# Expert rows gathered and scattered by indirect DMAs through HBM, in place of 0/1 products

## The chip, the cores and the metric

The kernel runs on one core of one Trainium2 chip. The metric is the device time of one execution in microseconds (us). An engine's work is told as the profile names it: PE is TensorE, DVE is VectorE, ACT is ScalarE, POOL is GpSimd, SP is SyncE, which here only issues DMAs.

## The reference, cut to what matters

The model has two layers. In each, 384 tokens (128 of a prompt, 256 latent ones) of width 1024 go through a mixer (pooling, attention, convolution) and then through a mixture of experts, which is where the change lies. A token is sent to 2 of 32 experts, both in the group that its router picks:

```python
g_w, g_idx = lax.top_k(softmax(t @ router_grp + b), 1)          # 1 of 4 groups
top_v, top_i = lax.top_k(e_logits[of that group], 2)            # 2 of its 8 experts
w = g_w * softmax(top_v)
h = silu(t @ w_gate[e]) * (t @ w_up[e])                         # 1024 -> 256
y = sum over both experts of  w * (h @ w_down[e])               # 256 -> 1024
x = layer_norm(ALPHA * x + gate2 * y)
```

All is float32. With the reference's inputs its routing gives, in the first layer, all 32 experts some rows, one of them more than 64 (72); in the second layer one expert has no row and three have more than 64 (87, 100 and 71).

## The kernel before

A token-expert assignment is a pair; there are 768. Pairs are sorted by expert. A chunk is up to 64 rows of one expert, and the list of chunks is made on the chip from the router's counts: `chunk_tab` holds each chunk's expert and its first column. Here it has 33 and 34 chunks, which the loops round up to 34 in each layer.

**Routing.** PE makes ranks of the pairs by products with a triangle of ones (`ranks_ready`, L870 and L872). VectorE turns them into sorted places `s1`, `s2` and builds the 0/1 matrix `Pm` (tokens by pairs, L1520 and L1521). **Gather.** PE multiplies the token rows `urow` by `Pm` (L907, 48 products), ScalarE and VectorE copy the result to `XsT`, the sorted rows as columns. Between, VectorE builds the weighted matrix `Pw` (L1575 to L1577), PE turns it (L892) and ScalarE stores it as `PTw`. SP waits for the chunk list (`chunks_ready`) and only then loads experts, each 3 MB (gate, up and down) into one of four slots of `ring`.

**Chunk loop.** For a chunk: `gate_up` (L928, 16 float32 products, each of two passes), silu by ScalarE (L1205), the product with the up half by VectorE (L1609), one transpose (L938), its copy to `hT` (L1611), `down` (L943), ScalarE's copy `take` to `yrow` (L1200), four transposes back to columns (L954) and a copy to `YsT` (L1618). In a round of four chunks PE issues gate_up of chunk i before down of chunk i-1, and ScalarE's silu of chunk i stands before its take of chunk i-1. Next to the copies, VectorE copies the inputs of a later chunk out of `XsT` (L1599). A slot is freed when down has read it, and SP then issues the next load into it.

**Unsort.** After the loop PE turns `YsT` to rows `Ysr` (L981) and multiplies them by `PTw` (L990, 48 products), which weights each pair and adds a token's two. VectorE adds this to the residual (L1446), PE sums for the layer norm (L822 and L827). The loads of the next layer's `w_mod` go on meanwhile.

Buffers of chunks alternate by `i % 2`, and semaphores that count chunks tell each engine when it may go on.

Of the kernel before, what the change touches and what calls it, by code (L numbers as in the profile page):

```python
# [25 lines left out]
ds = bass.ds  # L26
# [29 lines left out]
PADDED = PAIRS + W  # L56
# [9 lines left out]
MAX_CHUNKS = NE + (PAIRS - NE) // W  # L66
MAX_ROUNDS = -(-MAX_CHUNKS // RING)
LISTED = MAX_ROUNDS * RING + 2
# [17 lines left out]
for _name, _n in VECS:  # L86
# [4 lines left out]
              ("rank", NE), ("kk", 1), ("rounds", MAX_ROUNDS), ("inv", 2 * POOL_N)]  # L91


def shape_constants():
# [21 lines left out]
    c["kk"] = np.arange(P)[:, None]  # L116
    c["rounds"] = np.tile(np.arange(MAX_ROUNDS) * RING, (P, 1))
# [8 lines left out]
    iota = np.concatenate([np.tile(np.arange(PAIRS), (P, 1)), c["tri"]], axis=1).astype(np.float32)  # L126
    lam = np.array([0.8 - 0.6 * math.exp(-0.3 * l) for l in range(DEPTH)])
    lam = np.stack([lam, 1.0 - lam], axis=-1)[:, None, :].repeat(P, axis=1).astype(np.float32)
    return table, iota, lam
# [28 lines left out]
DVE_STEPS = 208  # L158


def build(nc, g, consts, iota_dram, lam_dram, y_prompt, y_sample, new_k, new_v):
    with ExitStack() as ctx:
# [11 lines left out]
        XS = max(KD * PADDED, NT * (D + PAIRS) + 2 * PAIRS)  # L174
        arena = sb("arena", [P, 2 * XS])
        PTw = sb("PTw", [P, ST, T])
# [18 lines left out]

        chunk_tab = sb("chunk_tab", [1, 2, LISTED], I32)
        rounds_tab = sb("rounds_tab", [1, 2, DEPTH], I32)
        before_f = sb("before_f", [1, 2, DEPTH + 1])
        before_tab = sb("before_tab", [1, 2, DEPTH + 1], I32)
# [36 lines left out]
        ptflat = PTw[:].rearrange("p s t -> p (s t)")  # L236
        sumX = ptflat[:, 0:2 * POOL_COLS].rearrange("p (c n) -> p c n", c=2)
        sumY = ptflat[:, 2 * POOL_COLS:4 * POOL_COLS].rearrange("p (c n) -> p c n", c=2)
        mrow = arena[:, 0:2 * HALF].rearrange("p (b n) -> p b n", b=2)

        XsT = arena[:, 0:KD * PADDED].rearrange("p (k n) -> p k n", k=KD)
        YsT = arena[:, XS:XS + KD * PADDED].rearrange("p (k n) -> p k n", k=KD)
        Ysr = arena[:, 0:ST * D].rearrange("p (s n) -> p s n", s=ST)
        urow = arena[:, XS:XS + NT * D].rearrange("p (t n) -> p t n", t=NT)
        Pm = arena[:, XS + NT * D:XS + NT * D + NT * PAIRS].rearrange("p (t n) -> p t n", t=NT)
        Pw = arena[:, XS + NT * (D + PAIRS):XS + NT * (D + PAIRS) + 2 * PAIRS].rearrange("p (t n) -> p t n", t=2)
        assert XS + NT * (D + PAIRS) + 2 * PAIRS <= 2 * XS
# [3 lines left out]
        sg = arena[:, KD * PADDED:KD * PADDED + FF].rearrange("p (b n) -> p b n", b=2)  # L251
        hrow = arena[:, XS + KD * PADDED:XS + KD * PADDED + FF].rearrange("p (b n) -> p b n", b=2)
        assert KD * PADDED + FF <= XS and 2 * W == P and FF == 2 * P
        hT = krow[:, 0:FF].rearrange("p (b n) -> p b n", b=2)
        iota_tri = tail[:, PAIRS:2 * PAIRS + P]
        iota, tri = iota_tri[:, 0:PAIRS], iota_tri[:, PAIRS:]
# [3 lines left out]
        RT_COLS = NT * (NG + NE) + NT * NG + 4 * NT * NE  # L260
# [10 lines left out]
        o1, o2 = rts(NT, NE), rts(NT, NE)  # L271
        etmp, asg = rts(NT, NE), rts(NT, NE)
        r3 = sb("r3", [P, 15, NT])
        gmax, gsum, gw, m1, m2, cm, q, s1, s2, w1, w2, rq, gcm, c1, c2 = [r3[:, i, :] for i in range(15)]
        assert at[0] == RT_COLS
        asg_flat = asg.rearrange("p t n -> p (t n)")
        lgT = arena[0:NG + NE, RT_COLS:RT_COLS + T]

        tot, start, cb, le, dd, ce = [tail[:, 2 * PAIRS + P + (NE + 1) * i:2 * PAIRS + P + (NE + 1) * (i + 1)] for i in range(6)]
        gtmp = tail[:, 2 * PAIRS + P + 6 * (NE + 1):][:, 0:NT * NG].rearrange("p (a b) -> p a b", a=NT)  # L280
        chk = sb("chk", [P, 4])
        small = sb("small", [P, 2, 2, 4])
        rnd = sb("rnd", [P, MAX_ROUNDS + 3])
# [27 lines left out]
        iota_loaded = signal("iota_loaded", 1, 16)  # L311
# [71 lines left out]
        chunk_cols = signal("chunk_columns", 1)  # L383
        chunk_turned = signal("chunk_turned", 1)
        chunks_ready = signal("chunk_list", 1)
        P_ready = signal("gather_matrix", 2 * NT)
        Pw_ready = signal("weighted_matrix", NT)
        Pw_turned = signal("weighted_turned", 2 * NT)
        PT_ready = signal("unsort_matrix", 2 * NT)
        gath_ready = signal("gathered", 2 * KD)  # L390
        xs_act = signal("sorted_x_act", KD)
        xs_dve = signal("sorted_x_dve", KD)


        xc_ready = signal("chunk_x_copied", 0)
        gu_ready = signal("gate_up_ready", 0, credit=4)
# [6 lines left out]
        y_turned = signal("y_turned", 0, credit=2)  # L403
        y_placed = signal("y_placed", 0, credit=2)
        ys_turned = signal("ys_turned", 12, credit=1)
        ys_act = signal("ys_rows_act", 6)
        ys_dve = signal("ys_rows_dve", 6)
# [1263 lines left out]
```

## Time and profile before

| what | value |
|---|---|
| median of 3 runs | 1259.55 us (1258.58 to 1259.93) |
| span of the profiled execution | 1257.7 us |
| PE busy (matmuls) | 1063.3 us, 85% |
| DVE, ACT, POOL busy | 419.7, 284.7, 32.8 us |
| moved by DMA | 300.36 MB, mean 239 GB/s |
| expert loads | 68 of each kind, 1024 KB each |

The profiled execution's own time is its span, 1257.7 us, and the median of the runs lies 1.85 us over it, for what surrounds the span. The page's chain of work says for each stretch of the span what it waited for last; windows give busy time by stretch. A busy PE is not a fast one: the chain and the gaps in the timeline tell what a stage really waits for.

### The profile page before, as it was taken

Reading aid. Unit: us, or ns where it says so; the run is one execution under the profiler, and the core shown is the slowest. Engines: PE = TensorE matmul, PEld = TensorE weight load, DVE = VectorE, ACT = ScalarE, POOL = GpSimd, SP = SyncE. Lnnn points to the kernel's source line nnn. Section 1 sums busy time; section 2 is a strip of 40 time slices with the busy share of each in tenths; the row PEclk is TensorE's granted clock in tenths of the full one; section 3 lists DMA queues with packets and bytes.
Section 4 is the critical chain, followed back from the end, with each engine's and each line's share of the span. In section 5 each row is a group of like instructions: output and inputs, shape, how many; then the busy total and the mean of one; then the engine's idle time right before and its main releaser. Section 6 shows DMA issues by size and latency. Waiting matters only on the chain.

```text
span 1257.7 us, 17279 instructions
## 1 busy us (share of the span) xinstructions
PE 1063.3 (85%) x5662; PEld 605.6 (48%) x5663; DVE 419.7 (33%) x1031; ACT 284.7 (23%) x638; POOL 32.8 (3%) x62
## 2 busy tenths in 40 slices
PE   2699988967888888888979998897789888888893
PEld 1256456534544444445535645653454444444552
DVE  0138553156122222223242854414712222222313
ACT  1200056042111111112050005704221111111304
POOL 4000000010000000000020000000000000000000
PEclk8799989988999999999989998998899999999997
DMA  9962530003799999996457244000189999999201
GB/s 344 394 227 87 193 122 1 1 16 115 314 418 419 416 417 419 418 417 264 188 170 300 101 164 154 2 0 15 72 331 403 417 418 418 417 417 419 94 1 50
DMA packets 70966, 300.36 MB, mean 239 GB/s; under 512 B 5381, under 2 KB 9763, under 8 KB 53505
## 3 DMA queue, kind: packets, MB, share of 16 engines
q1 hardware_dynamic: 68144, 293.98, 58.7%
q0 software_dynamic: 2768, 5.71, 1.4%
q8 instruction: 28, 0.46, 0.2%
q14 instruction: 26, 0.21, 0.1%
HBM read 297.05 MB, written 2.62 MB: 238 GB/s over the span
## 4 chain that ended last, share of the span: by engine, by line
PE 65%; DMA 20%; DVE 6%; issue 3%; SPq 3%; ACT 2%; DVEq 0%; ACTq 0%; POOL 0%
DMA ring<-in_w_down 17%; PE ps L660 12%; PE ps L928 9%; PE ps L943 7%; PE ps L840 7%; PE ps L907 5%; PE ps L990 5%; PE ps L663 3%; PE ps L625 3%; PE ps L827 2%; SPq L475 2%; DMA ring<-in_w_mod 2%; PE ps L822 2%; PE ps L954 1%; PE ps L762 1%
## 5 line engine op out<-in xcount | busy, mean ns | idle before, releaser
L928 PE MATMUL ps<-ring,tail 128*64 128x256 f32 x2176 | 248.5, 384 | 23.8 <-DMA ring<-in_w_down 14.6
L928 PEld LDWEIGHTS ps<-ring,tail 128*64 128x64 f32 x2176 | 166.0, 138 | 105.0 <-issue 43.5
L660 PE MATMUL ps<-uT,ring 128*128 128x384 f32 x448 | 152.5, 499 | 6.6 <-DMA ring<-in_w_in 5.0
L943 PE MATMUL ps<-ring,krow 128*64 128x512 f32 x544 | 131.7, 605 | 26.1 <-DVE krow L1611 26.1
L660 PEld LDWEIGHTS ps<-uT,ring 128*128 128x128 f32 x448 | 86.7, 195 | 64.8 <-issue 5.9
L1200 ACT ACTIVATE tail<-ps 128x512 f32<-128x512 f32 x68 | 40.6, 597 | 183.2 <-PE ps L943 183.2
L1611 DVE COPY krow<-ps 128x128 f32<-128x128 f32 x68 | 19.8, 292 | 176.9 <-PE ps L938 176.9
L907 PE MATMUL ps<-arena 128*128 128x512 f32 (+1 forms) x192 | 67.4, 507 | 11.5 <-DVE arena L1521 11.5
L1618 DVE COPY arena<-ps 128x512 f32 x68 | 47.1, 692 | 86.8 <-PE ps L954 86.8
L1446 DVE SCALAR_TENSOR_TENSOR uT<-ps,modT,uT 128x128 f32<-128x128 f32 x64 | 23.8, 413 | 148.9 <-PE ps L840 88.7
L625 PE MATMUL ps<-ring,sT 128*32 128x384 f32 x512 | 47.9, 530 | 27.7 <-DMA ring<-in_w_mod 24.2
L943 PEld LDWEIGHTS ps<-ring,krow 128*64 128x64 f32 x544 | 33.0, 136 | 77.9 <-DVE krow L1611 39.0
L1323 DVE SCALAR_TENSOR_TENSOR arena<-arena,dw 128x414 f32<-128x414 f32 x118 | 67.6, 646 | 0.0
L990 PE MATMUL ps<-PTw,arena 128*128 128x384 f32 x192 | 64.4, 487 | 1.8 <-DVE arena L1638 1.8
L840 PE MATMUL ps<-arena,ring 128*128 128x384 f32 x192 | 63.6, 486 | 0.0
L1205 ACT ACTIVATE arena<-ps 128x128 f32<-128x128 f32 x68 | 18.8, 277 | 163.6 <-PE ps L928 163.4
L907 PEld LDWEIGHTS ps<-arena 128*128 128x128 f32 x192 | 37.1, 198 | 38.1 <-issue 23.8
L954 PEld LDWEIGHTS ps<-cst,tail 128*128 128x128 f32 x272 | 28.5, 141 | 49.1 <-issue 40.6
L1147 ACT ACTIVATE arena<-uT 128x384 f32<-128x384 f32 x32 | 15.1, 523 | 157.3 <-DVE uT L1452 157.3
L990 PEld LDWEIGHTS ps<-PTw,arena 128*128 128x128 f32 x192 | 36.3, 190 | 27.1 <-ACT arena L1219 2.2
L840 PEld LDWEIGHTS ps<-arena,ring 128*128 128x128 f32 x192 | 36.5, 190 | 25.4
L954 PE MATMUL ps<-cst,tail 128*128 128x128 f32 x272 | 44.6, 287 | 4.2 <-ACT tail L1200 4.2
(257 smaller groups left out, 1009.2 us busy)
## 6 DMA issues: line engine op xcount, KB each, us to landing
ring<-in_w_gate SPq DMA_DIRECT2D x68, 1024.0 KB, 10.7
ring<-in_w_up SPq DMA_DIRECT2D x68, 1024.0 KB, 12.8
ring<-in_w_down SPq DMA_DIRECT2D x68, 1024.0 KB, 14.9
ring<-in_w_mod SPq DMA_DIRECT2D x32, 1536.0 KB, 10.9
ring<-in_w_in SPq DMA_DIRECT2D x8, 1536.0 KB, 15.1
ring<-in_w_out SPq DMA_DIRECT2D x4, 1536.0 KB, 19.0
ring<-in_w_in SPq DMA_DIRECT2D x2, 2048.0 KB, 13.1
ring<-in_w_in SPq DMA_DIRECT2D x4, 512.0 KB, 12.7
```

The lines of the kernel that those rows point to most:

```text
L625: last = mm(ps[32 * g_:32 * (g_ + 1), bank, 0:HALF], both, slot[s][:, k, (g_ % 2) * HALF:(g_ % 2 + 1) * HALF], start=(k == 0), stop=(k == ...
L660: last = mm(ps[:, n % 4, 0:T], slot[s][:, k, c:c + P], uT[:, k, :], start=(k == 0), stop=(k == KD - 1))
L663: last = mm(ps[:, n % 4, 0:AW], uT[:, k, rows * P:(rows + 1) * P], slot[s][:, k, c:c + AW], start=(k == 0), stop=(k == KD - 1))
L840: last = mm(ps[:, m % 4, 0:T], wt, mixT[:, k, :], start=(k == 0), stop=(k == KD - 1))
L907: last = mm(ps[:, n % 4, 0:b - a], urow[:, t, k * P:(k + 1) * P], Pm[:, t, a:b], start=(t == 0), stop=(t == NT - 1))
L928: last = mm(ps[W * half:W * (half + 1), i % 2, 0:2 * P].rearrange("p (j f) -> p j f", j=2), xc[:, i % 2, k, :], gate_up_w[i][:, :, k, half ...
L943: last = mm(ps[W * half:W * (half + 1), 3 + i % 2, :], hT[:, i % 2, f * W:(f + 1) * W], down_w[i][:, f, half * 512:(half + 1) * 512], star ...
L954: last = tr(ps[:, 5 + i % 2, c * P:(c + 1) * P], yrow[:, i % 2, c * P:(c + 1) * P], ident)
L990: last = mm(ps[:, m % 4, 0:T], Ysr[:, s, m * P:(m + 1) * P], PTw[:, s, :], start=(s == 0), stop=(s == ST - 1))
L1200: fn(yrow[:, i % 2, :], ps[:, 3 + i % 2, :], ID).then_inc(y_rows.sem, 1)
L1323: conv_own.append(own.add(v.scalar_tensor_tensor(cacc[:, c, :], src, wt, cacc[:, c, :], ALU.mult, ALU.add)))
L1618: v.tensor_copy(YsT[:, :, ds(off, W)].rearrange("p (h c) n -> p h c n", h=2), ps[:, 5 + i % 2, :].rearrange("p (c h n) -> p h c n", c=4, h ...
```

## The change

The 0/1 products go. Token rows are stored to a scratch in HBM, `u_rows` (768 rows of 512 floats, so a token has two). Two products of one-hot matrices (L938 of the new kernel) make `row_idx`: for each chunk the row numbers to read and the row numbers of `y_pairs` to write; places without a pair get a number out of bounds, which the DMA skips. For each chunk GpSimd issues one indirect DMA that fetches up to 128 half rows into `xg` (`fetch`) and one that writes `yrow` to `y_pairs` (`put`). PE turns `xg` to columns (`turn_x`, four transposes), in place of the four that turned y. After the loop ScalarE's queue loads `y_pairs` (3 DMAs of 1 MB), VectorE weights and adds a token's two rows, PE turns the sum (24 transposes), and the residual follows as before.

The chunk list becomes fixed: experts 0 to 31 in eight rounds of four, whether they have rows or not, and SP may load them before routing is known. Rows over 64 of an expert go to extra chunks, in turns of two; at least one turn runs. The loop over layers is written out. In the main loop PE's, ScalarE's and GpSimd's part read:

```diff
+def fetch(idx, done, half, i):                      # GpSimd
+    pool.wait_ge(x_turned.sem, done + (i + 1))
+    pool.nop(nofuse=True)
+    pool.indirect_dma_start(xg[:, i % 2, :], None, u_rows, bass.IndirectOffsetOnAxis(ap=idx, axis=0),
+                            bounds_check=2 * T - 1, oob_is_err=False).then_inc(xg_loaded[i % 2].sem, 16)
+def put(idx, done, half, i, first=False):
+    pool.wait_ge(y_rows.sem, done + (i + 3))
+    pool.nop(nofuse=True)
+    pool.indirect_dma_start(y_pairs, bass.IndirectOffsetOnAxis(ap=idx, axis=0), yrow[:, i % 2, :], None,
+                            bounds_check=4 * T - 1, oob_is_err=False).then_inc(y_stored[i % 2].sem, 16)
+def freed(half, i):
+    pool.wait_ge(y_stored[i % 2].sem, (half + (i // 2 + 1)) * 16)
+    pool.sem_inc(y_free.sem, 1)
+for i in range(2):
+    fetch(row_idx[:, i:i + 1], done, half, i)
+for i in range(NE):
+    if i + 2 < NE:
+        fetch(row_idx[:, i + 2:i + 3], done, half, i + 2)
+    put(row_idx[:, CHUNKS + i:CHUNKS + i + 1], done, half, i)
+    if i >= 1:
+        freed(half, i - 1)
...
+def chunk(done, half, used, i, ahead, follow):      # PE
+    turn_h(done, i)
+    if ahead:
+        turn_x(done, half, i + 2)
+    down(done, i, i % RING)
+    if follow:
+        gate_up(done, used((i + 1) % RING) + (i + 1) // RING, i + 1, (i + 1) % RING)
...
+with act.Fori(0, MAIN_ROUNDS - 1) as r:             # ScalarE
+    for i in range(RING):
+        silu(done + r * RING, i + 1)
+        take(done + r * RING, lambda s: slot_before(s) + r, i)
...
+with pool.Fori(0, turns) as r:                      # extra chunks, GpSimd
+    for i in range(2):
+        nc.gpsimd.tensor_copy(extra_idx[:, i, 0:1], row_idx[:, ds(NE + (r * 2 + i), 1)])
+        nc.gpsimd.tensor_copy(extra_idx[:, i, 1:2], row_idx[:, ds(CHUNKS + NE + (r * 2 + i), 1)])
...
+for t in range(NT):                                 # ScalarE's queue, then VectorE
+    act.dma_start(yk[:, t, :], y_pairs.rearrange("(t q r) n -> t q (r n)", t=NT, r=4)[t]).then_inc(y_loaded[t].sem, 16)
...
+    step(v.tensor_scalar(ysum[:, t, :], yk[:, t, D:2 * D], w2[:, t:t + 1], None, ALU.mult))
+    v.scalar_tensor_tensor(ysum[:, t, :], yk[:, t, 0:D], w1[:, t:t + 1], ysum[:, t, :], ALU.mult, ALU.add)
```

PE in the middle of a round, before: gate_up of chunk 2, then the transpose (L938) and down (L943) of chunk 1, the transposes of y (L954) of chunk 0, then gate_up of chunk 3.

```order
L924 REGISTER_ALU [waits expert_loaded2]
L928 MATMUL ps<-ring,tail 64x256 [waits h_rows_ready,chunk_x_copied]
L928 MATMUL ps<-ring,tail 64x256 x15
L936 REGISTER_ALU
L938 MATMUL ps<-cst,arena 128x128 [waits h_columns_ready,h_rows_ready]
L943 MATMUL ps<-ring,krow 64x512 [waits y_rows_copied,h_columns_ready]
L943 MATMUL ps<-ring,krow 64x512 x3
L954 MATMUL ps<-cst,tail 128x128 [waits y_placed,y_rows_copied]
L954 MATMUL ps<-cst,tail 128x128 x3
L924 REGISTER_ALU [waits expert_loaded3]
L928 MATMUL ps<-ring,tail 64x256 [waits h_rows_ready,chunk_x_copied]
```

And in the new kernel: gate_up of chunk 2 (L959), then the transpose (L968) of the same chunk, the transposes of x (L949) of the chunk two further on, down (L976) of chunk 2, and gate_up of chunk 3.

```order
L955 REGISTER_ALU [waits expert_loaded2]
L959 MATMUL ps<-ring,tail 64x256 [waits h_rows_ready,chunk_x_copied]
L959 MATMUL ps<-ring,tail 64x256 x15
L968 MATMUL ps<-cst,arena 128x128 [waits h_columns_ready,h_rows_ready]
L946 ISA
L949 MATMUL ps<-cst,pool_sums 128x128 [waits chunk_x_copied,chunk_x_rows0]
L949 MATMUL ps<-cst,pool_sums 128x128 x3
L976 MATMUL ps<-ring,krow 64x512 [waits y_rows_copied,h_columns_ready]
L976 MATMUL ps<-ring,krow 64x512 x3
L955 REGISTER_ALU [waits expert_loaded3]
L959 MATMUL ps<-ring,tail 64x256 [waits h_rows_ready,chunk_x_copied]
```

Between a chunk's gate_up and its own down no longer stands another chunk's gate_up, and the transposes of x, which wait for a fetch (`chunk_x_rows0`), stand ahead of down.

ScalarE in the new kernel: silu (L1208) of the next chunk, then take (L1215) of this one, whose down PE has ended before that next gate_up. Before, the order of the two in the code was the same, but take's down was issued after the gate_up of the silu ahead of it.

```order
L1206 REGISTER_ALU
L1208 ACTIVATE arena<-ps 128x128 [waits h_rows_ready,gate_up_ready]
L1215 ACTIVATE tail<-ps 128x512 [waits y_rows_free,slot_done2,down_half_ready]
L1206 REGISTER_ALU
L1208 ACTIVATE arena<-ps 128x128 [waits h_rows_ready,gate_up_ready]
L1213 REGISTER_ALU [waits down_half_ready]
L1215 ACTIVATE tail<-ps 128x512 [waits y_rows_free,slot_done3]
```

GpSimd in the new kernel has all fetches (L593) and puts (L600) in one row, one of each for a chunk: the fetch of chunk i+2, then the put of chunk i. Before, it had no instruction in this stage.

```order
L593 DMA pool_sums<-u_rows,row_idx 128x512 [waits y_rows_stored0,chunk_x_turned]
L600 DMA y_pairs<-tail,row_idx 1536x512 [waits y_rows_copied]
L593 DMA pool_sums<-u_rows,row_idx 128x512 [waits y_rows_stored1,chunk_x_turned]
L600 DMA y_pairs<-tail,row_idx 1536x512 [waits y_rows_copied]
L593 DMA pool_sums<-u_rows,row_idx 128x512 [waits y_rows_stored0,chunk_x_turned]
L600 DMA y_pairs<-tail,row_idx 1536x512 [waits y_rows_copied]
```

What moved: a fetch stands behind the put of the chunk three before its own.

## Rows read from the trace of the kernel before

**Rows 1.** The page: span, part 4 by engine, one group of part 5.

```profile
span 1257.7 us, 17279 instructions
...
PE 65%; DMA 20%; DVE 6%; issue 3%; SPq 3%; ACT 2%; DVEq 0%; ACTq 0%; POOL 0%
...
L1618 DVE COPY arena<-ps 128x512 f32 x68 | 47.1, 692 | 86.8 <-PE ps L954 86.8
```

**Rows 2.** Windows: busy us of each engine, granted clock, DMA share, GB/s.

```profile
389.00:569.00 180.00, 154.34 (x1082) 84.41 (x1082) 39.12 (x97) 28.68 (x54) 0.00 (x0) 1.00 1.02 418
```

**Rows 3.** The chain that ended last, in order of time: start, us, what.

```profile
330.74 8.56 PE ps L928 x64
...
348.50 3.60 PE ps L928 x32
...
448.14 18.09 DMA ring<-in_w_down
...
478.29 18.04 DMA ring<-in_w_down
...
579.35 1.95 PE ps L943 x7
...
625.99 0.93 PE ps L822 x2
...
1180.45 1.94 PE ps L943 x8
```

**Rows 4.** The timeline of one stretch of the chunk loop: start, us, engine, line.

```profile
474.09 0.28 DVE L1609 TENSOR_TENSOR arena<-arena,ps 128x128 f32<-128x128 f32 x1
...
474.42 0.33 PE L938 MATMUL ps<-cst,arena 128*128 128x128 f32 x1 [1.08 <-DVE arena L1609]
474.79 0.29 DVE L1611 COPY krow<-ps 128x128 f32<-128x128 f32 x1 [0.42 <-PE ps L938]
...
475.13 1.94 PE L943 MATMUL ps<-ring,krow 128*64 128x512 f32 x8 [0.38 <-DVE krow L1611]
...
477.00 0.66 PE L954 MATMUL ps<-cst,tail 128*128 128x128 f32 x4
477.24 0.60 ACT L1200 ACTIVATE tail<-ps 128x512 f32<-128x512 f32 x1 [3.72 <-PE ps L943]
...
483.83 0.28 ACT L1205 ACTIVATE arena<-ps 128x128 f32<-128x128 f32 x1
484.14 0.29 DVE L1609 TENSOR_TENSOR arena<-arena,ps 128x128 f32<-128x128 f32 x1 [4.75 <-ACT arena L1205]
```

**Rows 5.** The timeline: a VectorE step, rank product, row of 768, residual.

```profile
284.16 0.26 DVE L1485 TENSOR_TENSOR arena<-arena,cst 128x96 f32<-128x96 f32 x1
...
285.65 1.15 PE L872 MATMUL ps<-arena,cst 128*128 128x96 f32 x6
...
305.50 0.96 DVE L1577 TENSOR_TENSOR arena<-arena,tail 128x768 f32<-128x768 f32 x1
...
594.24 0.74 DVE L1446 SCALAR_TENSOR_TENSOR uT<-ps,modT,uT 128x128 f32<-128x128 f32 x2 [4.37 <-PE ps L990]
```

**Rows 6.** The timeline of GpSimd, and the copy that released it.

```profile
647.63 0.91 POOL L559 DMA_DIRECT2D router_w<-in_router_grp  x1
...
1245.42 0.60 ACT L1229 ACTIVATE arena<-ps 128x512 f32<-128x512 f32 x1 [0.26 <-PE ps L1002]
...
1246.31 0.54 POOL L577 DMA_DIRECT2D out<-arena  x1 [389.43 <-ACT arena L1229]
```

**Rows 7.** DMA issues at 250:265 and 640:655: count, KB each, us to landing.

```profile
vec_rows<-in_conv_ln_b POOLq DMA_DIRECT2D x1, 1.0 KB, 1.6
...
arena<-in_cache_k POOLq DMA_DIRECT2D x1, 256.0 KB, 3.0
...
conv_pw<-in_conv_pw POOLq DMA_DIRECT2D x1, 256.0 KB, 6.3
router_w<-in_router_exp POOLq DMA_DIRECT2D x1, 128.0 KB, 6.6
```

More of the change, by code:

```diff
@@ L55 @@
 W = 64
-PADDED = PAIRS + W
 RING = 4
@@ L90 @@
 CONST_COLS = [("ident", P), ("ones", P), ("rot", P), ("cos", LAT), ("sin", LAT),
-              ("rank", NE), ("kk", 1), ("rounds", MAX_ROUNDS), ("inv", 2 * POOL_N)]
+              ("rank", NE), ("turns", MAX_TURNS), ("inv", 2 * POOL_N), ("tri", P), ("place", P),
+              ("chunk", CHUNKS), ("sixty_fours", STEPS_64), ("tok", 2 * NT), ("tok_rank", 2 * NT), ("row", 1)]
 def shape_constants():
@@ L976, in _ @@
[L976 to L985 removed]
+                wait(idx_ready, l, 1)
@@ new lines, in _ @@
+                gate_up(done, slot_before(0), 0, 0)
+                with pe.Fori(0, MAIN_ROUNDS - 1) as r:
+                    for i in range(RING):
+                        chunk(done + r * RING, half + r * (RING // 2), lambda s: slot_before(s) + r, i, True, True)
+                last_done, last_half = done + (NE - RING), half + (NE - RING) // 2
+                for i in range(RING):
+                    chunk(last_done, last_half, lambda s: slot_before(s) + (MAIN_ROUNDS - 1), i, i + 2 < RING, i + 1 < RING)
@@ new lines, in _ @@
+                wait(chunks_ready, l, 1)
+                turns = turns_now(pe, l)
+                with pe.Fori(0, turns) as r:
+                    at_done, at_half = before * RING + NE + (turns_before + r) * 2, (before * RING + NE) // 2 + (turns_before + r)
+                    used = lambda s: slot_before(s) + (MAIN_ROUNDS + r)
+                    for i in range(2):
+                        turn_x(at_done, at_half, i)
+                    gate_up(at_done, used(0), 0, 0)
+                    for i in range(2):
+                        chunk(at_done, at_half, used, i, False, i == 0)
@@ L986, in _ @@
+                wait(y_sum, l, NT)
                 for m in range(KD):
@@ new lines, in _ @@
+                for i in range(RING):
+                    if i + 1 < RING:
+                        silu(done + (NE - RING), i + 1)
+                    take(done + (NE - RING), lambda s: slot_before(s) + (MAIN_ROUNDS - 1), i)
+                wait(chunks_ready, l, 1)
+                turns = turns_now(act, l)
+                with act.Fori(0, turns) as r:
+                    at_done = before * RING + NE + (turns_before + r) * 2
+                    silu(at_done, 0)
+                    silu(at_done, 1)
+                    for i in range(2):
+                        take(at_done, lambda s: slot_before(s) + (MAIN_ROUNDS + r), i)
@@ L1220, in _ @@
+                for b in range(2):
+                    act.wait_ge(y_stored[b].sem, ((before * RING + NE) // 2 + (turns_before + turns)) * 16)
+                for t in range(NT):
+                    act.dma_start(yk[:, t, :], y_pairs.rearrange("(t q r) n -> t q (r n)", t=NT, r=4)[t]).then_inc(y_loaded[t].sem, 16)
                 scale_x()
@@ new lines, in chunk @@
+                def chunk(done, i, ahead, follow):
+                    columns(done, i)
+                    if ahead:
+                        copy_x(done, i + 2)
+                    if follow:
+                        hidden(done, i + 1)
+                done = before * RING + turns_before * 2
+                for i in range(2):
+                    copy_x(done, i)
+                hidden(done, 0)
+                with dve.Fori(0, MAIN_ROUNDS - 1) as r:
+                    for i in range(RING):
+                        chunk(done + r * RING, i, True, True)
@@ new lines, in _ @@
+                for i in range(RING):
+                    chunk(done + (NE - RING), i, i + 2 < RING, i + 1 < RING)
+                wait(chunks_ready, l, 1)
+                turns = turns_now(dve, l)
+                with dve.Fori(0, turns) as r:
+                    at_done = before * RING + NE + (turns_before + r) * 2
+                    for i in range(2):
+                        copy_x(at_done, i)
+                    hidden(at_done, 0)
+                    for i in range(2):
+                        chunk(at_done, i, False, i == 0)
```

589 lines of the change are left out of this document (250 added, 339 removed).

## The prediction

> **What bounds the kernel now.** I read the page, then the chain of waits, then windows, then the timeline of the chunk loop. The page gives the span, 1257.7 us, with PE on 65% of the chain and DMA on 20% [rows 1]. The 68 copies of L1618 [rows 1] are 68 chunks, 34 a layer. The chain [rows 3] shows the expert stage of the first layer: the loop begins at 330.7 and its last down ends at 581.3, 250.6 us; then come the unsort and the layer norm, whose first sums end at 626.9, 45.6 us later. The last down of the second layer ends 601.1 us after that of the first, so the second repeats the first. Inside the loop the same wait for `ring<-in_w_down` comes every 30.15 us [rows 3]: four chunks, 7.54 us each. The window says why: DMA share 1.02 at 418 GB/s [rows 2], and 3.146 MB at 418 GB/s take 7.53 us. So the loop is bound by weight loads, but PE is close behind, busy 154.3 of 180 us there. A change can gain ahead of the loop and behind it; within it, it can only keep 7.5 us a chunk or lose.
>
> **Ahead of the loop.** The rank product ends at 286.8 [rows 5]. New until the first gate_up: some 20 steps of VectorE, 13 small ones at 0.26 us, six of 192 to 264 elements that I put at 0.45, one of 768 at 0.96 [rows 5], together 6.5 us with some overlap; 12 passes on PE, by 1.15 us for six [rows 5] 2.3 us; three steps, 0.9; GpSimd's start 0.29 after its release (1246.31 less the copy's end, 1246.02) [rows 6]; a fetch of up to 256 KB, 3.0 us when nothing else runs [rows 7]; 0.9 more for the second one's issue; four transposes 0.66 [rows 4] and a copy 0.69 [rows 1]. The loop starts near 301, not 330.7: a gain of 29.7 us a layer. The weights of four chunks are in by then, since SP no longer waits for the list.
>
> **A chunk in the loop.** PE alone: gate_up 3.60 [rows 3]; then silu and the product until PE starts, 483.83 to 484.43 and 0.05, that is 0.65; the transpose 0.33, the four of x 0.66 (the copy to `hT` lies under them), down 1.94 [rows 4]. Sum 7.2 us, which alone would cost nothing against 7.54. But the order of the new kernel closes a ring. fetch(i+3) stands on GpSimd behind put(i); put(i) waits for take(i); take(i) stands on ScalarE behind silu(i+1), which waits for gate_up(i+1). PE needs fetch(i+3) two small steps later, ahead of down(i+1), and everything of PE is queued behind that wait. Counted from the end of gate_up(i+1): silu and take 0.96 with their gaps (0.28 and 0.60 [rows 4]), GpSimd's start 0.29 [rows 6], the issue of put, the fetch from its start to landing, 0.05 to PE. PE arrives at 0.65 + 0.33 = 0.98. The stall is 0.3 us plus put's issue plus the fetch.
>
> Neither indirect DMA is in the trace. Put's issue: a plain one takes 0.54 us, one of 1024 pieces 0.91 [rows 6]; I take 0.91, as addresses must be read one by one. The fetch: 1.6 us for 1 KB on a quiet chip, 3.0 for 256 KB just before a weight load, 6.3 and 6.6 beside one [rows 7]. A freed slot's load starts with the end of down and takes 7.5 us; the fetch starts 3.6 + 0.96 + 0.3 + 0.9 = 5.8 us after that, so it runs beside the load for its first half only, and about a third of its rows exist: I take 4.0. The stall is then 0.3 + 0.9 + 4.0 = 5.2 us, with bounds of 0.3 + 0.5 + 1.6 = 2.4 and 0.3 + 0.9 + 6.6 = 7.8.
>
> For the fetch there is a page's price. The Trainium skill, "DMA: Bandwidth & Descriptors", section "Anatomy of one DMA", gives GpSimd's DMAs a fixed cost of about 2.0 us plus the bytes at 436 GB/s, which makes 2.6 us for 256 KB; the trace has 3.0 to 6.6. By the page the stall would be 3.8 us and the time, as an estimate, 1427 us.
>
> It comes 29 times a layer (chunks 3 to 31; the first three are fetched early, the last two chunks have none behind them). Main loop: 32 x 7.2 + 29 x 5.2 = 381 us. Weights cost nothing here, as 7.5 us of load fit into 12.4. VectorE's copies of x take the place of those to `YsT`, of the same size.
>
> **Extra chunks.** The first layer has one, the second three, so one turn and two turns of two chunks. A turn starts only when all puts have landed: take 0.6, put 0.3 + 4.0, the count read 1.0, four small copies 0.8, GpSimd's start 0.3 and two fetches 4.9, transposes and copy 1.35: 13.3 us in which PE stands. (The two small costs are estimates, by the smallest steps [rows 4, 5].) Then two chunks without overlap, 3.60 + 0.65 + 0.33 + 0.34 + 1.94 = 6.9 each. A turn is 27 us.
>
> **Behind the loop.** From the last down: take and put 4.9, ScalarE's issue 0.4, then 3 MB. Alone these are 2.5 us each at 418 GB/s after 2 us, the last at 9.5; in the first layer they share the DMA engines with 12 MB of `w_mod`, so I double the 2.5: 17. The last weighted sum is two steps over 1024 elements, by 0.96 for 768 [rows 5] 2.6 us. The eight turned tiles are paced by 0.74 of VectorE [rows 5] and 0.5 + 0.93 of PE [rows 3, 4], 1.5 each, 12. So 36.9 us in the first layer and 29.4 in the second, against 45.6: 8.7 and 16.2 gained.
>
> **The sum.** First layer: 381.4 + 27 - 250.6 = +157.8. Second: 381.4 + 54 - 250.6 = +184.8. Ahead: 2 x -29.7 = -59.4. Behind: -24.9. Together +258.3, span 1516.0; the median stood 1.85 over the span, so 1518 us.
>
> **Rivals.**
> - The stall is hidden and the loop stays bound by weights. For it: PE has 7.2 us of own work against 7.54. 28 further loads at 7.53 plus the rows (768 pairs, 4 KB each way, 6.3 MB a layer, 0.44 us a chunk) end the loop 144 us a layer earlier than above: 1230 us, faster. It decides where put's issue and the fetch together stay under about 0.5 us (258.3 over 58 stalls is 4.45 us off the 5.2). The smallest rows give 2.1. Chance 0.03.
> - Cheap DMAs: tiny ones as on a quiet chip, stall 2.4. 58 x 2.8 = 162, and 16 from three turns: 1340 us. For it: two thirds of the rows are skipped. Against it: any fetch with data on the DMA engines took 3.0. Chance 0.08 for all below 1400.
> - Dear DMAs: the fetch is as slow as beside a load, 6.6, stall 7.8: 58 x 2.6 + 16 more, 1685 us. If GpSimd needs twice 0.91 for each index list, 52 and more on top, 1740. For it: the indices lie in 128 partitions, and no row shows what that costs. Chance 0.17 for above 1620.
> - My forecast, 1400 to 1620 us: 0.72.
>
> **How the numbers follow.** The forecast is the likeliest case. The range 1400 to 1690 leaves out both lower cases (0.11) and the end of the dear one (0.07). A measurement here tells 0.2% from no change; every case but the first is slower, so faster 0.03, same 0.01, slower 0.96.
>
> **What the profile after would show.** If the ring is right: in the chain a repeated sequence of gate_up, silu, take, put, fetch, transposes, down; PE idle some 5 us a chunk ahead of the transposes of x, released by the DMA into `pool_sums`; a round of four near 50 us; DMA at about 60% in the loop and 250 GB/s, not 418; GpSimd busy about 2 us a chunk. The loop starts near 301, the first turn shows PE idle for 13 us. The forecast is wrong if PE's wait stands elsewhere, if rounds stay at 30 us, if GpSimd itself is busy most of the period, or if skipped rows cost as much as real ones.

## The result, and the profile after

The changed kernel took 1699.6 us (median of 4 runs) against 1259.7 us: a ratio of 1.350 (95% interval 1.348 to 1.352). The forecast was 1518 us with a range up to 1690; the sign and the place were right, the size was not. One of the four runs of experiment 1, 1327.6 us, lies over 1.5% above its fastest and is left out of its figures; with it the median is 1307.9 us, from which the expectation of experiment 5 starts. The page of the kernel after, its span, chain by engine, and the group of the transposes of x (busy us, mean ns of one, idle time before it and what ended most of it), to set beside [rows 1]:

```profile
span 1696.7 us, 14958 instructions
...
PE 60%; DMA 19%; issue 7%; DVE 4%; ACT 4%; POOL 3%; SPq 2%; POOLq 1%; ACTq 0%; DVEq 0%
...
L949 PE MATMUL ps<-cst,pool_sums 128*128 128x128 f32 x280 | 76.5, 429 | 405.0 <-DMA pool_sums<-u_rows,row_idx 372.1
```

405 us of PE's idle time stand ahead of one line, and 372 of them are ended by the gather into `pool_sums`. So the added time has an address. The window over the main loop of the first layer, to set beside [rows 2]:

```profile
332.00:770.00 438.00, 242.84 (x1298) 116.68 (x1299) 35.60 (x84) 21.76 (x56) 57.49 (x57) 0.72 0.56 218
```

The DMA share is 0.56 in place of 1.02 and 218 GB/s in place of 418: the weights no longer bound the loop. GpSimd, the last of the five pairs, is busy 57 of 438 us, so no engine bounds it either; it is a ring of waits. The figure behind the pairs, the granted clock, is 0.72, and it was 1.00 before. The chain of the kernel after, from the end of one gate_up to the next (start, us, what), where the chain of before had `ring<-in_w_down` every 30.15 us [rows 3]:

```profile
439.26 0.05 ACT arena L1208
439.43 0.04 issue
439.48 0.61 ACT tail L1215
440.18 0.53 issue
440.73 0.07 issue
440.92 1.01 POOL y_pairs L600
441.93 0.30 issue
442.24 4.46 DMA pool_sums<-u_rows,row_idx
446.69 0.04 issue
446.74 1.11 PE ps L949 x4
```

This is the ring that the prediction named, read from top to bottom: SiLU, take, put, fetch, transposes. Three of its pieces can be laid beside the forecast's. Between the take's end (439.48 + 0.61 = 440.09) and the put's start (440.92) lie 0.83 us, not 0.29. The put's issue is 1.01 us, not 0.91, and 0.30 us follow it before the fetch starts. The fetch lands 4.46 us after its start here (5.13 in the chunk before, median 4.3 over the loop, 3.6 to 5.1), against 4.0.

The fourth piece is PE itself. Windows of the chunk before this one (length, busy us of PE, PEld, DVE, ACT and POOL, granted clock, DMA share, GB/s): the wait, the transposes with the first half of down, its second half, and the two halves of gate_up.

```profile
423.90:430.80 6.90, 0.00 (x0) 0.00 (x0) 0.26 (x1) 0.00 (x0) 2.02 (x2) 0.61 0.89 353
430.90:433.00 2.10, 2.10 (x8) 1.15 (x10) 0.69 (x1) 0.00 (x0) 0.00 (x0) 0.50 0.00 0
433.00:435.40 2.40, 2.40 (x10) 0.55 (x8) 0.00 (x0) 0.00 (x0) 0.00 (x0) 0.50 0.00 0
435.40:437.40 2.00, 2.00 (x20) 1.35 (x18) 0.00 (x0) 0.00 (x0) 0.00 (x0) 0.94 0.20 25
437.40:439.40 2.00, 1.73 (x17) 0.84 (x12) 0.00 (x0) 0.14 (x1) 0.00 (x0) 1.00 0.96 397
```

PE's timeline in the same stretch, the transposes and down:

```profile
430.88 1.11 PE L949 MATMUL ps<-cst,pool_sums 128*128 128x128 f32 x4 [7.04 <-DMA pool_sums<-u_rows,row_idx]
431.92 3.68 PE L976 MATMUL ps<-ring,krow 128*64 128x512 f32 x8
```

In the 6.9 us in which PE stands the granted clock falls to its lower level, 1.2 GHz (0.61 is the mean of the wait, 0.50 the figure of its last 4.9 us), and it stays there through the transposes and nearly all of down; it is back at 2.4 GHz in gate_up. The down products took 3.68 us here and 1.94 before [rows 4], the transposes 1.11 and 0.66. No DMA runs beside them (share 0.00), so it is not traffic that slows them. So the wait is paid a second time, in the work behind it.

The rest, from the timeline of PE:

| | forecast | measured |
|---|---|---|
| first gate_up of the first layer | 301 | 302.4 |
| main loop, first gate_up to last down | 381, 381 | 471.6, 475.3 |
| turn of the first layer | 27 | 26.2 |
| two turns of the second | 54 | 57.5 |
| last down to the last sum of the norm | 36.9, 29.4 | 37.8, 27.6 |
| from there to the first gate_up of the second layer (304.5 before) | 274.8 | 265.8 |

The two main loops are 184 us over their terms. The other differences nearly cancel, and the miss is 182: the second layer's first gate_up comes 9 us sooner than forecast, the rest is up to 3.5 us a line. A chunk with a stall takes 15.5 us (29 of them from 311.1 to 760.2), not 12.4.

### The profile page after: what moved, and what is told of

Its sections match the earlier page's. It is cut to its first block, busy times and chain, and to the rows that moved or that the text cites. A ratio compares the mean times of both kernels' runs of the same rounds, so it can differ in the third digit from the quotient of the medians.

```text
span 1696.7 us, 14958 instructions
## 1 busy us (share of the span) xinstructions
PE 1075.4 (63%) x5304; PEld 573.3 (34%) x5304; DVE 369.6 (22%) x890; ACT 241.1 (14%) x587; POOL 180.2 (11%) x219
## 3 DMA queue, kind: packets, MB, share of 16 engines
q0 software_dynamic: 14672, 20.57, 3.4%
## 4 chain that ended last, share of the span: by engine, by line
PE 60%; DMA 19%; issue 7%; DVE 4%; ACT 4%; POOL 3%; SPq 2%; POOLq 1%; ACTq 0%; DVEq 0%
PE ps L959 16%; DMA pool_sums<-u_rows,row_idx 15%; PE ps L976 13%; PE ps L721 9%; PE ps L901 5%; PE ps L949 4%; POOL y_pairs L600 3%; PE ps L724 2%; ACT tail L1215 2%; PE ps L686 2%; SPq L483 1%; DMA arena<-y_pairs 1%; PE ps L883 1%; PE ps L888 1%; DMA ring<-in_w_mod 1%
## 5 line engine op out<-in xcount | busy, mean ns | idle before, releaser
L949 PE MATMUL ps<-cst,pool_sums 128*128 128x128 f32 x280 | 76.5, 429 | 405.0 <-DMA pool_sums<-u_rows,row_idx 372.1
L959 PE MATMUL ps<-ring,tail 128*64 128x256 f32 x2240 | 275.3, 402 | 0.0
L976 PE MATMUL ps<-ring,krow 128*64 128x512 f32 x560 | 223.6, 944 | 3.8 <-DVE krow L1593 3.8
L959 PEld LDWEIGHTS ps<-ring,tail 128*64 128x64 f32 x2240 | 172.1, 150 | 151.3 <-issue 83.1
L949 PEld LDWEIGHTS ps<-cst,pool_sums 128*128 128x128 f32 x280 | 49.6, 215 | 420.6 <-DMA pool_sums<-u_rows,row_idx 373.3
L1208 ACT ACTIVATE arena<-ps 128x128 f32<-128x128 f32 x70 | 19.4, 278 | 971.0 <-PE ps L959 971.0
L600 POOL DMA_INDIRECT y_pairs<-tail,row_idx x64 | 64.6, 1010 | 808.6 <-ACT tail L1215 781.1
L1581 DVE COPY tail<-ps 128x512 f32<-128x512 f32 x70 | 48.4, 692 | 462.5 <-PE ps L949 462.5
L1588 DVE TENSOR_TENSOR arena<-arena,ps 128x128 f32<-128x128 f32 x70 | 20.1, 288 | 455.2 <-ACT arena L1208 455.2
L976 PEld LDWEIGHTS ps<-ring,krow 128*64 128x64 f32 x560 | 50.4, 204 | 103.6 <-issue 97.5
L593 POOL DMA_INDIRECT pool_sums<-u_rows,row_idx x64 | 65.0, 1016 | 42.9 <-issue 28.9
L968 PE MATMUL ps<-cst,arena 128*128 128x128 f32 x70 | 22.9, 327 | 55.4 <-DVE arena L1588 55.4
L1215 ACT ACTIVATE tail<-ps 128x512 f32<-128x512 f32 x70 | 41.5, 593 | 13.3 <-PE ps L976 13.3
L724 PE MATMUL ps<-ring,uT 128*128 128x512 f32 x96 | 42.1, 594 | 0.0
L968 PEld LDWEIGHTS ps<-cst,arena 128*128 128x128 f32 x70 | 9.7, 138 | 87.1 <-DVE arena L1588 67.3
## 6 DMA issues: line engine op xcount, KB each, us to landing
ring<-in_w_in SPq DMA_DIRECT2D x2, 2048.0 KB, 11.3
```

The costliest lines, as they stand in the source:

```text
L593: pool.indirect_dma_start(xg[:, i % 2, :], None, u_rows, bass.IndirectOffsetOnAxis(ap=idx, axis=0), bounds_check=2 * T - 1, oob_is_err=Fal ...
L600: pool.indirect_dma_start(y_pairs, bass.IndirectOffsetOnAxis(ap=idx, axis=0), yrow[:, i % 2, :], None, bounds_check=4 * T - 1, oob_is_err= ...
L724: last = mm(ps[:, n % 4, 0:AW], uT[:, k, rows * P:(rows + 1) * P], slot[s][:, k, c:c + AW], start=(k == 0), stop=(k == KD - 1))
L949: last = tr(ps[:, 5 + i % 2, c * P:(c + 1) * P], xg[:, i % 2, c * P:(c + 1) * P], ident)
L959: last = mm(ps[W * half:W * (half + 1), i % 2, 0:2 * P].rearrange("p (j f) -> p j f", j=2), xc[:, i % 2, k, :], gate_up_w[s][:, :, k, half ...
L976: last = mm(ps[W * half:W * (half + 1), 3 + i % 2, :], hT[:, i % 2, f * W:(f + 1) * W], down_w[s][:, f, half * 512:(half + 1) * 512], star ...
```

## The experiments

Times "alone" are a single run beside runs of the kernel before; the others are medians of four, in experiment 1 of three. In the diffs, `silu`, `take`, `fetch` and `put` are the calls of the prediction.

**1. The ring cut on GpSimd.** Three chunks are fetched at the start, and fetch(i+3) stands ahead of put(i).

```diff
-    if i + 2 < NE:
-        fetch(row_idx[:, i + 2:i + 3], done, half, i + 2)
+    if i + 3 < NE:
+        fetch(row_idx[:, i + 3:i + 4], done, half, i + 3)
     put(row_idx[:, CHUNKS + i:CHUNKS + i + 1], done, half, i)
```

> GpSimd issues the fetch of chunk i+3 ahead of the put of chunk i instead of behind it; nothing else differs. Theory A (the ring put, fetch, transposes, down, gate_up, take, put sets the pace): the fetch has a whole chunk more, the stall of 7.0 us ahead of the transposes of x goes, the loop is bound by weights again at 7.5 to 8.0 us a chunk, the main loop takes 240 to 255 us instead of 471 and the median falls to 1235 to 1265 us. Rival B (indirect DMAs are slow or disturb the weight loads whatever the order): the DMA engines or GpSimd stay the bound, over 10 us a chunk, over 1400 us.

Measured: 1304.6 us, ratio 1.037 (1.031 to 1.043), above the 1235 to 1265 of theory A and far below rival B's 1400. One reordered call takes away 395 us of the 440 with the same DMAs in it: their order was the cause. But it isn't the kernel without a ring. GpSimd's timeline there:

```profile
425.78 1.01 POOL L600 DMA_INDIRECT y_pairs<-tail,row_idx  x1 [8.06 <-PE ps L949]
427.10 1.01 POOL L593 DMA_INDIRECT pool_sums<-u_rows,row_idx  x1 [0.30 <-issue]
432.61 1.01 POOL L600 DMA_INDIRECT y_pairs<-tail,row_idx  x1 [4.50 <-DMA y_pairs<-tail,row_idx]
433.92 1.01 POOL L593 DMA_INDIRECT pool_sums<-u_rows,row_idx  x1 [0.31 <-issue]
443.25 1.01 POOL L600 DMA_INDIRECT y_pairs<-tail,row_idx  x1 [8.32 <-PE ps L949]
444.56 1.01 POOL L593 DMA_INDIRECT pool_sums<-u_rows,row_idx  x1 [0.30 <-issue]
```

The brackets give the idle time before and what the profile takes for its end. For the puts they mislead: the chain has the take ahead of them (424.34 to 424.95 for the put of 425.78), with the same 0.83 us between. So a fetch still starts right behind a late put each time, and the fetch of 427.10 landed only at 433.97, as it now runs beside a weight load (median 6.4 us, where it was 4.3). Chunks alternate: one goes through in 6.9 us, the next waits and takes 10 or 11.

**2. The take ahead of the SiLU,** GpSimd's order as in the changed kernel. ScalarE copies the rows of chunk i out while PE does gate_up(i+1).

```diff
-    silu(done + r * RING, i + 1)
     take(done + r * RING, lambda s: slot_before(s) + r, i)
+    silu(done + r * RING, i + 1)
```

> ScalarE copies y of chunk i (take) ahead of the silu of chunk i+1; GpSimd's order stays as in the changed kernel. Theory A: the ring loses gate_up and silu, the put starts about 4 us earlier, the stall shrinks from 7.0 to about 3 us: 29 x 2 x 4 = 233 us less and some of the slow clock back, 1400 to 1460 us. Rival B: no more than 20 us less, since the DMAs themselves set the pace.

Measured: 1598.0 us alone, above the 1400 to 1460 expected. The put starts 1.6 us after the end of down in place of 5.3, but the chunk falls only from 15.5 to 13.7 us: the fetch now starts 2.7 us after the first issue of the weight load (427.20 and 424.55) instead of 6.4 (442.24 and 435.86), and its median landing is 6.3 us. The transfer moved beside another gives back 2.0 of the 3.7 us that the move gains.

**3. PE kept busy in the wait.** Twelve products of 128x256 that nothing reads, ahead of the wait for the gathered rows; nothing else changes.

```diff
     pe.wait_ge(xc_ready.sem, done + (i + 1))
+    for _ in range(12):
+        mm(ps[:, 5 + i % 2, 0:LAT], ident, C["cos"], start=True, stop=True)
     pe.wait_ge(xg_loaded[i % 2].sem, (half + (i // 2 + 1)) * 16)
```

> The changed kernel, with 12 products of no use (128x128 by 256 columns, into a bank that the transposes overwrite) put on PE ahead of each wait for a fetch in the main loop, 5.2 us at the full clock, less than the stall of 7.0. Theory C (PE stands, the granted clock falls to half, and about 1.1 us of each chunk's 15.4 are PE's own work at the slower clock): the clock stays near 1.0, down takes 1.94 us again instead of up to 3.7, a chunk takes 14.2 to 14.6 us, 1620 to 1655 us. Rival D (the slow down and gate_up come of contention with DMA writes, not of the clock): durations stay, and the time is 1697 or more.

Measured: 1604.8 us alone, 95 less than the changed kernel, by adding work; theory C holds, and its 1620 to 1655 was too cautious. PE's timeline after the wait:

```profile
439.44 0.66 PE L951 MATMUL ps<-cst,pool_sums 128*128 128x128 f32 x4 [1.44 <-DMA pool_sums<-u_rows,row_idx]
440.03 1.94 PE L978 MATMUL ps<-ring,krow 128*64 128x512 f32 x8
```

Transposes and down are back at the times of [rows 4], and the window 332 to 700 has a granted clock of 0.99. A chunk takes 13.7 us (29 from 315.2 to 712.9). The 1.8 us between this and 15.5 are what the full clock gives back, some 104 us in 58 chunks; 10 of them are lost again in the first chunk of each layer, where the useless products stand and no wait was. The wait for the gather stays.

**4. Plain DMAs in place of the indirect ones.** Put and fetch move 128 fixed rows each. The experts get other tokens' rows, so the output isn't the reference's.

```diff
-    pool.indirect_dma_start(xg[:, i % 2, :], None, u_rows, ...)
+    pool.dma_start(xg[:, i % 2, :], u_rows[0:P, :])
```

> Fetch and put are plain GpSimd DMAs of 128 fixed rows, in the same places and with the same waits; the experts so get rows that are not theirs, and all 128 rows of a chunk move instead of about a third. Theory A with the index list as a small term: put's issue 0.54 us instead of 1.01, the fetch's issue likewise, its landing a little later for three times the bytes: 0.5 to 1.0 us a chunk less, 1640 to 1680 us. Rival E (the index lists are the dear part): the fetch lands in 2.5 us or less and the time falls below 1600.

Measured: 1744.1 us alone, slower than the changed kernel. The timeline of ScalarE's copy and of GpSimd in this kernel:

```profile
445.20 0.60 ACT L1213 ACTIVATE tail<-ps 128x512 f32<-128x512 f32 x1
...
446.34 0.54 POOL L599 DMA_DIRECT2D y_pairs<-tail  x1 [14.10 <-ACT tail L1213]
446.92 0.54 POOL L593 DMA_DIRECT2D pool_sums<-u_rows  x1
```

And its DMA issues in the window 340 to 700 (count, KB each, median us to landing):

```profile
y_pairs<-tail POOLq DMA_DIRECT2D x22, 256.0 KB, 6.1
pool_sums<-u_rows POOLq DMA_DIRECT2D x22, 256.0 KB, 6.0
```

The issue is 0.54 instead of 1.01 us and the gap of 0.30 is gone, 0.74 us less from the put's start to the fetch's; the put itself starts 0.54 us after the copy in place of 0.83. But the landing goes from 4.3 to 6.0, which is more than both savings. My expectation held the issue for the larger of the two and was wrong. So the index lists are not what made the changed kernel slow. Whether the longer landing comes from the bytes (each DMA moves all 256 KB) or from the earlier start (5.3 us after the load's first issue, 446.92 and 441.66, in place of 6.4), this run doesn't separate; experiment 10 bears on it.

**5. Both reorderings,** with two buffers.

> Both reorderings at once: GpSimd gathers chunk i+3 ahead of putting chunk i back, and ScalarE copies the rows of a chunk out ahead of the next chunk's SiLU. With the gather first alone the median was 1307.9 us and the chunks alternated between 6.9 and 10.5 us. Theory P: the gathers still queue behind puts on GpSimd, and the puts are late because the copy waits behind the SiLU; then an earlier copy moves the loop towards the weights' own 7.5 to 8.3 us per chunk: 1265 to 1285 us. Theory Q: the two buffers of gathered rows are what holds (a gather can't start before the chunk two before it is turned, and lands 6 to 8 us later beside the weights); then an earlier copy changes little: 1298 to 1312 us.

Measured: 1269.2 us, ratio 1.008 (1.006 to 1.010). The earlier copy, worth 102 us by itself, is worth 35 here. Theory P holds: the puts were late, and the two buffers were enough.

**6 and 7. Four buffers of gathered rows,** in order of the changed kernel on ScalarE (6) and with the earlier copy (7). Two of them lie in a part of `arena` that is free during the loop; fetch(i+4) waits for the turn of chunk i.

```diff
-    fetch(row_idx[:, i + 2:i + 3], done, half, i + 2)
+    fetch(row_idx[:, i + 4:i + 5], done, i + 3, i + 4)
     put(row_idx[:, CHUNKS + i:CHUNKS + i + 1], done, half, i)
```

> Four buffers of gathered rows in place of two, and four gathers issued ahead: gather i+4 waits for the turn of chunk i and stands ahead of put i on GpSimd. ScalarE's order as in the changed kernel. Theory Q (the two buffers were the ring): the loop is bound by the transfers, weights 3.15 MB and rows about 0.3 MB per chunk at the 418 GB/s that the weights had in the kernel before, so 8.2 to 8.4 us per chunk, main loop 264 to 270 us in place of 471.6, total 1260 to 1280 us with a granted clock above 0.9. Theory R: the gathers' landing grows with their number in flight, or the way from the put to the free row buffer is a second ring of 8.6 us or more: main loop 275 us or more, total 1300 us or more.

> Four buffers of gathered rows as in the run before, and ScalarE copies the rows of a chunk out ahead of the next chunk's SiLU. If the loop of the run before is bound by the transfers, an earlier put gives nothing: within 5 us of it. If the puts are in its ring: 15 to 30 us less. If the SiLU is now what is late on TensorE's path: up to 10 us more.

Measured: 1269.2 us (ratio 1.009, 1.007 to 1.010) and 1268.3 us (1.008, 1.007 to 1.010). Three different kernels (5, 6 and 7) within 1 us of each other are at a common bound; 6 falls into the range of theory Q, but as 5 gets there with two buffers, the buffers were not what held. The window 426 to 541 of the kernel with four buffers:

```profile
426.00:541.00 115.00, 88.87 (x630) 49.90 (x630) 17.78 (x42) 10.88 (x28) 26.21 (x26) 1.00 1.02 412
```

PE's timeline in it:

```profile
426.47 3.67 PE L960 MATMUL ps<-ring,tail 128*64 128x256 f32 x32 [1.23 <-DMA ring<-in_w_down]
430.92 0.33 PE L969 MATMUL ps<-cst,arena 128*128 128x128 f32 x1 [0.77 <-DVE arena L1589]
431.14 0.63 PE L950 MATMUL ps<-cst,arena 128*128 128x128 f32 x4
431.70 1.94 PE L977 MATMUL ps<-ring,krow 128*64 128x512 f32 x8
```

Share 1.02, clock 1.00, and the wait is for `in_w_down` again, as in [rows 3]; nothing stands ahead of the transposes any more. A chunk takes 8.2 us where the kernel before had 7.54: the rows now share the engines with the weights. The gather's own landing is 6.8 us here and costs nothing.

**8. The first turn folded into the fixed loop,** on top of 6. It always runs; its two chunks become chunks 32 and 33, with the experts read from the list, and only later turns stay behind the drain.

```diff
-    for i in range(RING):
-        chunk(last_done, ..., i, i + 2 < RING, i + 1 < RING)
+    for i in range(RING + 2):
+        chunk(last_done, ..., i, i < RING, i + 1 < RING + 2)
...
-    with pe.Fori(0, turns) as r:
+    with pe.If_ne(pe.to_reg(turns), 1):
+        with pe.Fori(1, turns) as r:
```

> Four buffers of gathered rows, and the two chunks of the first turn, which always runs, are done as chunks 32 and 33 of the fixed loop, in place of after it has drained; only turns from the second on stay in the loop of their own. A drained turn took 26.2 to 30.8 us from the last product of the loop; two more chunks of a loop without a drain take 2 times 8.3, so 10 us less per layer: 20 us less than the run with four buffers alone, so 1240 to 1260 us if that one falls at 1260 to 1280, and then level with the kernel before or 1 per cent faster. If the drain is hidden behind the weights of the turn anyway: no gain.

Measured: 1241.2 us, ratio 0.986 (0.984 to 0.988): 1.4% under the kernel before, and the gain over 6 is 28 us where 20 were expected. The first layer's last down ends at 572.8, 8.5 us before that of [rows 3].

**9. The list waited for.** As 8, but SyncE waits for the tables before the first expert's load, as the kernel before did.

```diff
+    wait(chunks_ready, l, 1, alone=True)
     with sp.Fori(0, MAIN_ROUNDS) as r:
         load_experts(RING, lambda i: r * RING + i, lambda i: slot_before(i) + r)
```

> As the run with four buffers and the folded first turn (1241.2 us), but SyncE waits for the tables of the layer before it loads the first expert, as the kernel before did: the order of the experts stays fixed. The tables are ready at 296.4 us of layer 1; the four buffers' weights were loaded by then in the folded run. Theory L (the loop is bound by the transfers, and the four experts loaded early are a head start of at most 4 times 7.5 us, of which the wait for the tables hides a part): 34 chunks at 8.24 us from 298 us end at 578 to 585 us in place of 572.8, so 6 to 12 us per layer: 1253 to 1266 us. Theory M (the whole advance of the first products before the kernel before, 29.7 us per layer, comes from the early loads): 1290 to 1302 us.

Measured: 1270.2 us, 29.1 more than 8, so 14.5 a layer: between the two theories, nearer to L. The first gate_up starts only 6.7 us later (309.8), but the last down of that layer ends 16.2 us later (589.0): where the transfers are the bound, loads begun early are paid out over the whole loop, not at its head. Theory L took too much of the four loads for hidden.

**10. No rows gathered.** As 8, with the bound of the gathers at 0, so that all rows but the first are skipped. The products read what the buffers hold; the output isn't the reference's.

```diff
-    bounds_check=2 * T - 1, oob_is_err=False).then_inc(xg_loaded[i % 4].sem, 16)
+    bounds_check=0, oob_is_err=False).then_inc(xg_loaded[i % 4].sem, 16)
```

> As the run with four buffers and the folded first turn (1241.2 us), but the gathers' bound is set so that every row but the first of the scratch is skipped: the same instructions and waits, without the 3.1 MB of rows per layer that they fetch. The products read what stands in the buffers, so the output is not the reference's. Theory S (the loop is bound by bytes): 3.1 MB at 412 GB/s is 7.6 us per layer: 1224 to 1230 us. Theory T (rows of 2 KB cost the engines more than their bytes beside the weights): the loop's 8.24 us per chunk against 7.54 before is 0.70 us for the rows of both ways, 0.35 of it the gathers', times 34: 12 us per layer, 1214 to 1220 us. Theory U (the products are the bound): no change, 1238 to 1244 us.

Measured: 1213.9 us, 27.3 less than 8, at the lower edge of theory T. GpSimd's DMA queue in 8 and in 10 (packets, MB, share of the DMA engines), and the landing of the gathers in 10:

```profile
q0 software_dynamic: 14672, 20.57, 4.7%
...
q0 software_dynamic: 14672, 14.30, 3.5%
...
pool_sums<-u_rows,row_idx POOLq DMA_INDIRECT x36, 6.5
```

6.27 MB at 412 GB/s are 15.2 us, 7.6 a layer. The main loop of the first layer is 11.8 us shorter, 1.6 times that; the 27.3 of the whole kernel are 1.8 times, but some of them lie outside the loops (the first gate_up comes 1.5 us sooner). So rows of 2 KB among the weights cost more than their bytes, as theory T has it. The same lines show what skipping a row saves: bytes, but no packet, and hardly any waiting. The count of packets is 14672 in both, and in experiment 4 too, where every row moved; and a gather with all rows but the first skipped still lands in 6.5 us beside the weights, against 6.8 to 6.9 in 8. That makes the bytes unlikely to be all of the longer landing in experiment 4, though no run shows their share.

**11. The simplest form of 8,** two buffers, both reorderings, folded turn.

> The two reorderings (gather of chunk i+3 ahead of the put of chunk i, copy out ahead of the next SiLU) with two buffers of rows, and the first turn folded into the fixed loop. With two and with four buffers the unfolded kernels took 1269.3 and 1269.2 us, so if the transfers bound both: 1238 to 1245 us, as with four buffers. If two buffers are just enough at 8.2 us per chunk but not through the change from the loop's experts to the listed ones: up to 1255 us.

Measured: 1241.6 us, ratio 0.986 (0.984 to 0.988). The second pair of buffers isn't needed.

**12 and 13. The sum of the two halves of the stall.** The changed kernel with the earlier copy and with 12, then with 8 products without use.

> The changed kernel with the copy out of a chunk's rows ahead of the next SiLU (alone 1598.0 us, 101.6 less) and 12 products of 128x256 without use ahead of each wait for the gathered rows (alone 1604.8 us, 94.8 less). The order in which GpSimd puts and gathers, and the ring, stay. If the start of the put and the clock are two separate terms of the chunk's 15.4 us, the two add: 1495 to 1515 us, which is where the forecast of 1518 us lay with its stall of 5.2 us and a full clock. If they are not separate (the products without use take the place of work that the earlier copy has uncovered, or the gather is late anyway beside the weights): 1530 to 1570 us.

> As the run with the earlier copy and 12 products without use ahead of the wait, but 8 of them, 3.5 us in place of 5.2. Theory V: the gather lands 6.3 us after its start (the median of the run with the earlier copy alone), so at 618.1 in a stretch where the 12 products ended at 618.6; then 8 leave a wait of about 1.2 us and the chunk falls from 12.04 to 11.5 us: 1480 to 1495 us, and what is left of the stall from the transpose of h is about 4.7 us. Theory X: the gather lands much earlier and the 12 products alone set the time: 10.4 us a chunk, 1410 to 1430 us. Theory Y: with fewer products the clock falls back: 1520 us or more.

Measured: 1514.9 us (ratio 1.204, 1.201 to 1.206) and 1497.1 us (1.190, 1.186 to 1.193), the second 2 us above its theory V. The chain of 12 in one chunk (start, us, what):

```profile
613.13 0.33 PE ps L970
613.46 5.18 PE ps L948 x24
618.64 0.44 PE ps L951 x4
619.08 1.87 PE ps L978 x8
```

It has the useless products (L948) in it and no wait for the gather, so its number lies at the forecast's by chance. In 13 the wait is back (start, us, what):

```profile
609.22 0.66 PE ps L951 x4
609.88 1.88 PE ps L978 x7
...
611.91 0.61 ACT tail L1217
...
613.35 1.01 POOL y_pairs L600
614.36 0.31 issue
614.67 6.00 DMA pool_sums<-u_rows,row_idx
620.67 0.04 issue
620.71 0.66 PE ps L951 x4
```

Here gate_up and SiLU are out of the ring; what is left is transposes, down, take, put and fetch, 11.5 us in this stretch, at the full clock, of which the two indirect DMAs hold 7.3.

## Why the prediction missed its size

- **What bounds the kernel, and where the ring lies:** right. The chain shows the predicted sequence, and cutting it at the predicted place (experiment 1) took away nine tenths of the loss.
- **Ahead, turns, behind:** right within 4 us each but one. The first gate_up came at 302.4 for 301, the turns took 26.2 and 57.5 for 27 and 54, the two ends 37.8 and 27.6 for 36.9 and 29.4. The second layer's first gate_up came 38.7 us sooner behind the first layer's norm, not 29.7; nearly all of the 9 us more lie ahead of the first products with `in_w_in`, for which PE waited 5.0 us before and 1.7 after. The turns were right in part by luck: up to their first gate_up the three took 11.3, 11.8 and 15.9 us for 13.3, and their two chunks 14.9 for 13.8, with a granted clock of 0.79 in the first 4.7 us.
- **The failed step is the sum of a chunk, 7.2 + 5.2 us, and above all the 7.2.** The chunk took 15.5. The 7.2 us of PE's own work came from rows at the full clock ([rows 2] has 1.00), and I carried them into a loop in which PE stands over 40% of the time. The wait ahead of the transposes, read from PE's timeline in all 58 chunks, is 6.2 us on the mean; the other 9.3 are PE's own work, 2.1 more than forecast. That is 58 x 2.1 = 122 us, the larger part. Experiment 3 shows the clock to be its cause. It gives back 1.8 us of the 2.1, as the wait is 6.5 us there (13.7 less 7.2), with a gather that lands about 0.2 us later. None of the rivals held this step, though the page already lists the granted clock beside each stage.
- **The stall's small terms.** The stall was 6.2, not 5.2: 58 x 1.0 = 58 us. The put's start after its release was 0.83 for 0.29 (+0.54); the row [rows 6] was one plain DMA elsewhere in the program. The put's issue was 1.01 for 0.91 (+0.10), and the gap of 0.30 between two indirect DMAs was in no term. These make 0.94, and the fetch's mean of 4.2 for 4.0 makes 1.14; PE came to the wait 1.09 us after gate_up in the chunk shown, not 0.98, which takes 0.11 off again and leaves the 1.0.
- **The fetch:** near in size, and half right in reason. That it runs beside the load for a part only did count: it took 6.3 to 6.8 us where it lay beside weight loads for its whole length (experiments 1, 2, 6), the upper bound of the estimate. That only a third of its rows exist counted for little by experiment 10 (6.5 us with none but the first row, 6.8 to 6.9 with all that exist). The page of the Trainium skill weighed there, "DMA: Bandwidth & Descriptors", section "Anatomy of one DMA", would have made 2.6 us, as an estimate; the fastest of the 29 fetches that PE waited for in the first loop landed in 3.6 us.
- **The rivals.** "Dear DMAs" gave 1685 to 1740 us, and the result lies there, but not by its cause: neither was the fetch 6.6 us in this kernel nor the issue twice 0.91. Experiment 4 took the index lists out and was slower. The hidden stall (1230 us) never was near for this order; as a different kernel, 8 and 11 come to it within 12 us.

The 122 and 58 us make 180 of the 184; the other 4 are the six chunks without a stall, of which the first of each layer took 8.8 and 10.6 us for 7.2, with a granted clock of 0.50 at its start. Of the 0.54 us that the put starts later than forecast, experiment 4 assigns about half: a plain put in the same place starts 0.54 us after its copy, the indirect one 0.83, a plain DMA elsewhere in the program 0.29. What of the place costs the other 0.25 stays open.

## What to carry to other kernels

Before an operation of several microseconds goes on a shared queue, write down which waits it stands behind there and which it stands ahead of: the same DMAs, in another order on GpSimd and ScalarE, took 1700 or 1269 us. When a forecast puts a wait of several microseconds in front of TensorE once a chunk, price its products at the lower clock too. And once nothing but the transfers bound a loop, ask for the bytes, for the drains (the folded turn gave 28 us) and for the loads that can start early (29 us), not for more buffers.

## What the runs showed of the hardware that I had not expected

- Behind a wait of 6.9 us without a product the granted clock was at 0.50 in the transposes and down (430.9 to 435.4), and at 0.94 in the 2.0 us that follow; with the 12 products in the wait it was 0.99 over the loop. Twelve useless products a chunk made the kernel 95 us faster.
- An indirect DMA of 128 indices held GpSimd for 1.01 us, and for 1.02 where all its rows but the first of the scratch were skipped (experiment 10). Two in a row lay 0.30 us apart; a plain one of 256 KB held it for 0.54, with 0.04 us to the next.
- An indirect put started 0.83 us after the copy that released it, a plain one in the same place 0.54 (experiment 4).
- Skipped rows saved bytes but no packets: 14672 packets on GpSimd's queue with all rows moved (experiment 4), with a part (experiment 8) and with almost none of the gathered ones (experiment 10).
- The gather's landing was 4.3 us when only its first part lay beside a weight load, 6.3 to 6.8 us when all of it did, and 6.5 us there even with all rows but the first skipped.
- Rows of 2 KB fetched beside the weight stream cost the loop 1.6 times the time of their bytes (11.8 us for 3.1 MB in the first layer, 7.6 by the 412 GB/s of the loop).
